# High and low weight matmuls taken in turn, block by block, in the up products of two feed-forward layers

## The chip, the cores and the metric

The kernel runs on one core of a Trainium2 chip. Its time is the device time of one execution in microseconds (us). Before the change it took 2998.19 us, the median of three executions (2997.39 to 3000.05). Every time below is of that kernel.

The matmuls go through TensorE (PE in the rows; PEld is its weight load). VectorE is DVE, ScalarE is ACT, GpSimd is POOL and SyncE, which issues the loads, is SP.

## The reference, cut to what matters

A stack of four layers runs over 256 tokens of 2048 features in float32: two of a first kind, then two of a second. Only the layers of the first kind have a feed-forward part:

```
def squared_relu_mlp(h, w_up, w_down):
    return jnp.square(jax.nn.relu(h @ w_up)) @ w_down

for layer in range(2):
    ...
    h = h + rmsnorm(mix, norm_mix_post[layer])
    f = squared_relu_mlp(rmsnorm(h, norm_mlp_pre[layer]), w_up[layer], w_down[layer])
    h = h + rmsnorm(f, norm_mlp_post[layer])
```

`w_up` is 2048 x 8192 and `w_down` 8192 x 2048. The rest (a gated mixer, a dilated attention, two layers with three kinds of attention) uses the same kind of product, and the change leaves it alone.

## The kernel before, in words

**Two halves of every number.** A float32 weight chunk is split into a rounded high part and a low part, the difference. The input is split in the same way. A product is high weight times high input, plus high weight times low input, plus low weight times high input. For each block of 128 input features (`kt`, 16 of them) that takes two matmuls:

- `high_unit` (line 306): weights `w_high`, and both halves of the input as 512 columns, into a whole bank of PSUM (`acc`).
- `low_unit` (line 313): weights `w_low`, and the high half of the input as 256 columns, added to the second half of the same bank.

VectorE then adds the two halves of the bank (`sum_halves`, line 1290), which gives the 128 output features of the chunk for 256 tokens.

**Chunks and slots.** The weights come as a stream of 512 chunks of 1 MB. Chunk c goes through slot c % 4 of `raw`, `w_high` and `w_low`. SyncE loads chunk c once product c - 4 is done. ScalarE rounds it (`high`, line 855) and VectorE subtracts (`low`, line 1281); both work three chunks ahead of the product that uses the chunk (`ahead`). TensorE waits by counters: `summed` (the bank has been read), `high_ready` and `low_ready` (the weights are split).

**The order inside a product.** `product` runs a pass over the 16 blocks with `w_high` and a pass over them with `w_low`. Without `flip` the high pass is first; with `flip` the low pass is first. In the up products of the feed-forward layers the odd slots are flipped, from the ninth product of the first quarter on, so that two low passes stand back to back and then two high passes.

**The feed-forward section.** `mlp_section` works in four quarters of the 8192 inner features. A quarter is 16 up products, one for each 128 inner features (in the first quarter four of the 16 come from an input group with wide tiles, and the next four are plain, unflipped products), and then an `out_section` of 16 wide chunks through `both_halves` (line 377), all of whose matmuls have 512 columns. After each up product VectorE adds the halves, scales, applies the squared relu and splits the result; then it does its `low` for the chunk three ahead.

The names that matter below: `product`, `high_unit`, `low_unit`, `high_ready`, `low_ready`, `summed`, `product_done`, and the call of `product` in `mlp_section`. All this order is written out by hand; no planner decides it.

Of the kernel before, what the change touches and what calls it, by code (L numbers as in the profile page):

```python
# [41 lines left out]
UNITS = 16  # L42
# [66 lines left out]
def build(nc, stream, x_t, x_rows, columns, gains_post, lambdas, w_spatial, b_spatial, positions, tables, out):  # L109
    ctx = ExitStack()  # L110
    with ctx:
# [5 lines left out]
        def sem(name):  # L117
            if name not in sems:
                sems[name] = ctx.enter_context(nc.semaphore(name))
            return sems[name]  # L120
# [115 lines left out]
        high_ready, low_ready = sem("high_ready"), sem("low_ready")  # L236
# [8 lines left out]
        def at(value):  # L245

            return max(value, 0)
# [55 lines left out]
        def _(pe):  # L303
            def high_unit(s, kt, x, bank=None, stop=False):

                return nc.tensor.matmul(acc[s if bank is None else bank][:, :], w_high[:, s, kt * P:(kt + 1) * P],  # L306
                                        x[:, kt, :, :], start=(kt == first_of[0]), stop=stop, skip_group_check=True)
# [3 lines left out]
            def low_unit(s, kt, x, stop, start=False, bank=None):  # L311

                return nc.tensor.matmul(acc[s if bank is None else bank][:, TOKENS:], w_low[:, s, kt * P:(kt + 1) * P], x[:, kt, 0, :],  # L313
                                        start=start, stop=stop, skip_group_check=True)

            def product(c, s, x, units=UNITS, hooks=None, bank=None, freed=None, order=None, flip=False):


                order = order or list(range(units))
                first_of[0] = None if flip else order[0]  # L320

                def high_pass():
                    pe.wait_ge(high_ready, c + 1)
                    for kt in order:
                        if hooks and kt in hooks:
                            hooks[kt]()
                        mm = high_unit(s, kt, x, bank, flip and kt == order[-1])
                    return mm

                def low_pass():  # L330
                    pe.wait_ge(low_ready, c + 1)
                    for kt in order:
                        mm = low_unit(s, kt, x, not flip and kt == order[-1], flip and kt == order[0], bank)
                    return mm
                pe.wait_ge(summed, at(c - 3) if freed is None else freed)
                if flip:
                    low_pass()
                    mm = high_pass()
                else:
                    high_pass()  # L340
                    mm = low_pass()
                mm.then_inc(product_done, 1)
# [126 lines left out]
            def input_group(c, n, banks, out0):  # L469


                m = n - 1
                at_turn = 4 if m % 2 and m < 4 else 1

                def first(half):
                    def ready(kt, part):
                        k = turned_at(half, kt // KT_WIDE)
                        pe.wait_ge(sem("xs_ready" if part else "xs_high"), inputs_at(n, k) - KT_WIDE + kt % KT_WIDE + 1)
                    return ready

                def second(kt, part):
                    k = turned_at(1, kt // KT_WIDE)
                    pe.wait_ge(sem("xs_ready" if part else "xs_high"), inputs_at(n, k) - KT_WIDE + kt % KT_WIDE + 1)
                pe.wait_ge(sem("rows_out"), out0 + TB * (GROUPS - 1))
                one_half(c, 0, 0, xs, banks, ready=first(0))
                one_half(c + 1, 1, 0, xs, banks, ready=first(0), hooks={at_turn: lambda: turn_rows(m, 2)})
                one_half(c, 0, 1, xs, banks, ready=first(1), hooks={at_turn: lambda: turn_rows(m, 3)}, low_last=False)\
                    .then_inc(product_done, 1)
                one_half(c + 1, 1, 1, xs, banks, ready=first(1), low_last=False,
                         hooks={4: lambda: turn_rows(m, 4), 8: lambda: turn_rows(m, 5)}).then_inc(product_done, 1)  # L490
                parts_apart(c + 2, 2, xs, banks, second,
                            hooks={8: lambda: (turn_rows(m, 6), turn_rows(m, 7))})
                parts_apart(c + 3, 3, xs, banks, second)
# [10 lines left out]
            def spread(r):  # L504

                pe.wait_ge(sem("root_ready"), r + 1)
                for n in range(TB):
                    mm = nc.tensor.matmul(extra[:, n * P:(n + 1) * P], root_of[:, n:n + 1].to_broadcast([P, P]), ident,  # L508
                                          start=True, stop=True, skip_group_check=True)
                mm.then_inc(sem("spread_done"), 1)  # L510
# [42 lines left out]
            def mlp_section(c0, split0, n, r, m, off, out0):  # L553
                def turn_up():
                    for half in range(TB):
                        pe.wait_ge(sem("up_squared"), TB * (m // 2) + half + 1)
                        for b in range(KT_WIDE):
                            mm = nc.tensor.transpose(score[half][:, b * P:(b + 1) * P],
                                                     v_four[:, half, b * P:(b + 1) * P], ident)
                        mm.then_inc(sem("up_turned"), 1)  # L560

                for q in range(FFN_QUARTERS):
                    c, before = c0 + 2 * KB * q, out0 + FINAL_GROUPS * (q - 1)
                    if q == 0:
                        input_group(c, n, (2 - off, 3 - off) if off == 0 else (0, 1), before)
                    for j in range(KT_WIDE if q == 0 else 0, KB):
                        s, hooks = j % 4, None
                        if q == 0 and j == KT_WIDE:
                            hooks = {4: lambda: spread(r)}
                        if q == 0 and j == KT_WIDE + 1:  # L570
                            hooks = {2: turn_up}
                        freed = None
                        if q == 0 and j < KT_WIDE + 2:
                            pe.wait_ge(sem("rows_out"), before + FINAL_GROUPS)
                            freed = c
                        if q and j < 4:
                            pe.wait_ge(sem("rows_out"), before + TB * (GROUPS - 1) + (TB if s > 1 else 0))
                            freed = c - KB
                        product(c + j, s, xs, bank=(s + off) % 4, freed=freed, hooks=hooks,
                                flip=s % 2 == 1 and (q > 0 or j > 7))  # L580
                    c = c + KB
                    out_section(c, m, split0 + KB * q, ((off, off + 1), (2 - off, 3 - off)), c - 2,
                                out0 + FINAL_GROUPS * q, last=q == FFN_QUARTERS - 1)

            for i, (a, b) in enumerate(FIRST_PIECES):
                last = b == KT_WIDE
                wide_high(0, 0, 0, xs, 0, units=range(a, b), high=None if last else (sem("first_high"), i + 1), xs_base=0)
                mm = wide_low(0, 0, 0, xs, 0, units=range(a, b), low=None if last else (sem("first_low"), i + 1))
# [39 lines left out]

            out_section(C_OUT0, 0, 0, ((0, 1), (2, 3)), C_OUT0 - 2, 0, MIX0_ORDER)
            mlp_section(C_MLP0, 16, 1, 1, 1, 2, FINAL_GROUPS)  # L630


# [8 lines left out]
            for i in range(HEADS // 4):  # L641
                c, off = C_QKV + 12 * i, 2 * (i % 2)
# [15 lines left out]
                for g in range(4):  # L658
                    hd, cq, s = 4 * i + g, c + 4 + 2 * g, 2 * g % 4
# [18 lines left out]
            for l in range(LAYERS):  # L678
# [25 lines left out]
                for hd in range(DA_HEADS):  # L704
                    for j in range(3):
                        p = 3 * hd + j
                        c = c0 + 4 + p
                        if p == 4:
                            pe.wait_ge(sem("v_four_ready"), TB * (HEADS // 4 + l + 1))
                        freed = c - 1 if p in (2, 3) else c - 2 if p == 5 else None  # L710
                        product(c, p % 4, xs, bank=query_banks.get(p, p % 4), freed=freed,
                                hooks={0: lambda: spread(r0)} if p == 1 else None)
# [11 lines left out]
                c, hd = c0 + N_DA, DA_HEADS - 1  # L724
# [14 lines left out]
                def window_turns(b):  # L739
                    for j in range(2):  # L740
                        turn_prob(u0 + 8 + 2 * b + j, j)
# [36 lines left out]
                c = c0 + N_DA + N_KV + N_SW  # L778
                for i in range(N_LATENT):
                    hooks = {1: {14: lambda: window_turns(SW_BLOCKS - 1)}, LATENT + 2: {4: lambda: spread(r0 + 5)}}  # L780
# [48 lines left out]
                c = c + N_LATENT  # L829
                for hd in range(MLA_HEADS):  # L830
                    hooks = {15: lambda: mla_scores(hd - 1)} if hd > 1 else {} if hd else {
                        4: lambda: latent_stat(N_LATENT - 2), 12: lambda: latent_stat(N_LATENT - 1)}
# [1332 lines left out]
```

## Time and profile before

| | |
|---|---|
| median of three executions | 2998.19 us |
| the profiled execution | 2997.29 us |
| its span on the core | 2995.3 us |
| TensorE matmul busy | 2975.1 us, 15768 matmuls |
| TensorE weight load busy | 2544.7 us |
| VectorE, ScalarE, GpSimd busy | 2033.6, 1412.1, 33.5 us |
| DMA | 554.42 MB, mean 185 GB/s |
| granted TensorE clock, whole span | 0.999 |

The busy time of TensorE is not the same as working at its peak: matmuls are pipelined, and the end of each is modelled, so that records of neighbours overlap. The distance between the starts of two matmuls is what counts. In a row of the timeline that merges n matmuls, it is the row's length less the length of one matmul, divided by n - 1; or, from one row to the next, the difference of the starts divided by the count. Weight loads overlap matmuls in the same way.

The chain of waits gives the share of each line of the work that ended last. The timeline shows the instructions in order of time. The groups by line give busy time, mean duration and the idle time ahead.

### The profile page before, as it was taken

The page shows a single profiled execution, that of the slowest core. Times are in us where ns is not written, and L with a number is a line of the kernel's source. Part 1 is how long each engine was busy: PE and PEld are TensorE (multiplying, and loading weights), DVE is VectorE, ACT ScalarE, POOL GpSimd, SP SyncE. Part 2 cuts the span into 40 slices and gives each one's busy share as a digit, 9 for nine tenths or more (in the row PEclk, how much of TensorE's full clock was granted, in tenths as well). Part 3 has the DMA queues.
Part 4 walks back from the last instruction along what each step waited for, and adds up shares of the span by engine and source line. Part 5 has one row for each costly group of instructions (what it writes and reads, how often), then busy time and mean ns, then how long its engine had stood idle before and what let it go on. Part 6 is the DMA issues. An engine that isn't in the chain of part 4 may idle for free.

```text
span 2995.3 us, 38044 instructions
## 1 busy us (share of the span) xinstructions
PE 2975.1 (99%) x15768; PEld 2544.7 (85%) x15768; DVE 2033.6 (68%) x2720; ACT 1412.1 (47%) x1798; POOL 33.5 (1%) x38
## 2 busy tenths in 40 slices
PE   9999999999999999999999999999999999999999
PEld 7888888888888788888888888888888888888887
DVE  7776765746566587775756657465689865789764
ACT  5334543434333465554533334343666644666543
POOL 0000000000000000000000000000000000000000
PEclk9999999999999999999999999999999999999999
DMA  7555455555555444445555555555444445444444
GB/s 267 215 184 204 175 189 191 194 189 192 195 186 210 171 181 170 177 180 192 182 188 191 194 188 195 193 187 211 170 168 169 156 159 193 182 172 152 169 157 166
DMA packets 81658, 554.42 MB, mean 185 GB/s; under 512 B 9040, under 2 KB 9552, under 8 KB 16080
## 3 DMA queue, kind: packets, MB, share of 16 engines
q1 hardware_dynamic: 81488, 552.00, 50.9%
q8 instruction: 125, 2.05, 0.3%
q14 instruction: 45, 0.37, 0.0%
HBM read 549.87 MB, written 2.10 MB: 184 GB/s over the span
## 4 chain that ended last, share of the span: by engine, by line
PE 97%; issue 1%; ACT 1%; DVE 1%; POOL 0%; DMA 0%; SPq 0%; DVEq 0%; POOLq 0%; ACTq 0%
PE acc L377 37%; PE acc L306 33%; PE acc L313 17%; PE acc L356 2%; PE score L518 2%; PE acc L366 1%; PE acc L802 1%; PE head_out L547 1%; PE score L526 1%; PE acc L809 1%; PE head_out L549 0%; PE score L436 0%; DMA raw<-stream 0%; PE extra L508 0%; DVE w_low L1281 0%
## 5 line engine op out<-in xcount | busy, mean ns | idle before, releaser
L1281 DVE TENSOR_TENSOR w_low<-raw,w_high 128x2048 fp32r<-128x2048 f32 x511 | 1163.9, 2280 | 537.2 <-ACT w_high L855 536.3
L855 ACT ACTIVATE w_high<-raw 128x2048 fp32r<-128x2048 f32 x511 | 974.7, 1909 | 1158.3 <-DMA raw<-stream 1158.0
L306 PE MATMUL acc<-xs,w_high 128*128 128x512 f32 x4322 | 1039.4, 393 | 0.0
L306 PEld LDWEIGHTS acc<-xs,w_high 128*128 128x128 f32 x4322 | 795.6, 188 | 163.5 <-issue 6.0
L377 PE MATMUL acc<-w_high,inner 128*128 128x512 f32 x3072 | 733.6, 390 | 0.0
L377 PEld LDWEIGHTS acc<-w_high,inner 128*128 128x128 f32 x3072 | 575.4, 188 | 118.6
L313 PEld LDWEIGHTS acc<-xs,w_low 128*128 128x128 f32 x4322 | 544.7, 191 | 15.5
L313 PE MATMUL acc<-xs,w_low 128*128 128x256 f32 x4322 | 549.5, 283 | 0.0
L377 PE MATMUL acc<-w_low,inner 128*128 128x512 f32 x1536 | 382.5, 390 | 0.0
L1290 DVE TENSOR_REDUCE y<-acc 128x256 f32<-128x512 f32 x272 | 187.5, 689 | 254.6 <-PE acc L313 148.9
L377 PEld LDWEIGHTS acc<-w_low,inner 128*128 128x128 f32 x1536 | 287.8, 188 | 60.2 <-issue 0.7
L935 ACT ACTIVATE inner<-source 128x256 fp32r<-128x256 f32 x168 | 69.8, 415 | 93.4 <-DVE source L1456 57.8
L987 ACT ACTIVATE swapped<-y 32x256 f32<-32x256 f32 (+1 forms) x208 | 86.5, 416 | 39.2 <-DVE y L1290 36.6
L994 ACT ACTIVATE prob<-prob,small 128x128 f32<-128x128 f32 (+1 forms) x144 | 64.5, 449 | 69.0 <-DVE small L1533 37.7
L1298 DVE TENSOR_TENSOR scaled<-y,scale_pre 128x256 f32<-128x256 f32 x192 | 81.6, 425 | 9.8
L356 PE MATMUL acc<-w_high,xs 128*128 128x512 f32 x320 | 80.4, 402 | 6.9 <-ACT w_high L1021 6.5
L377 PE MATMUL acc<-w_high,xs 128*128 128x512 f32 x320 | 82.9, 397 | 0.0
L356 PEld LDWEIGHTS acc<-w_high,xs 128*128 128x128 f32 x320 | 60.2, 192 | 19.6 <-ACT w_high L1021 6.5
L1420 DVE TENSOR_TENSOR inner<-source,inner 128x256 fp32r<-128x256 f32 x168 | 70.2, 418 | 1.0 <-ACT inner L935 1.0
L377 PEld LDWEIGHTS acc<-w_high,xs 128*128 128x128 f32 x320 | 58.3, 188 | 13.3 <-issue 1.9
L1456 DVE SCALAR_TENSOR_TENSOR source<-scaled 128x256 f32<-128x256 f32 x120 | 51.0, 425 | 4.1
L1361 DVE SCALAR_TENSOR_TENSOR xs<-score,col,xs 128x128 fp32r<-128x128 f32 x120 | 33.7, 343 | 18.5 <-ACT xs L877 18.5
(177 smaller groups left out, 1401.9 us busy)
## 6 DMA issues: line engine op xcount, KB each, us to landing
raw<-stream SPq DMA_DIRECT2D x511, 1024.0 KB, 4.8
gain<-gains_post SPq DMA_DIRECT2D x24, 256.0 KB, 5.0
h<-x_rows SPq DMA_DIRECT2D x8, 256.0 KB, 5.1
out<-h SPq DMA_DIRECT2D x8, 256.0 KB, 2.1
x_in<-x_t SPq DMA_DIRECT2D x3, 512.0 KB, 9.8
consts<-tables SPq DMA_DIRECT2D x1, 960.0 KB, 15.7
x_in<-x_t SPq DMA_DIRECT2D x2, 256.0 KB, 4.3
raw<-stream SPq DMA_DIRECT2D x2, 256.0 KB, 4.4
```

The costliest lines, as they stand in the source:

```text
L306: return nc.tensor.matmul(acc[s if bank is None else bank][:, :], w_high[:, s, kt * P:(kt + 1) * P], x[:, kt, :, :], start=(kt == first_of ...
L313: return nc.tensor.matmul(acc[s if bank is None else bank][:, TOKENS:], w_low[:, s, kt * P:(kt + 1) * P], x[:, kt, 0, :], start=start, sto ...
L356: mm = nc.tensor.matmul(acc[bank + n][:, :], x[:, kt, part, n * P:(n + 1) * P], w_high[:, s, a * WIDE:(a + 1) * WIDE], start=(kt == 0 and ...
L377: return nc.tensor.matmul(acc[bank][:, :], x[:, kt, part, rows(n)], w[:, s, a * WIDE:(a + 1) * WIDE], start=start, stop=stop, skip_group_c ...
L855: nc.scalar.activation(w_high[:, s, 0:units * P], raw[:, s, 0:units * P], ACT.Copy)\
L935: nc.scalar.activation(inner[:, b, 0], source[:, s, :], ACT.Copy).then_inc(sem("inner_high"), 1)
L987: cp = nc.scalar.activation(to[a:a + half, :], src[b:b + half, :], ACT.Copy)
L994: nc.scalar.activation(prob[:, bank, lo:hi], prob[:, bank, lo:hi], ACT.Exp, bias=neg_max(bank, t), accum_out=denom(bank, t)).then_inc(sem( ...
L1281: V.tensor_tensor(w_low[:, s, 0:units * P], raw[:, s, 0:units * P], w_high[:, s, 0:units * P], ALU.subtract).then_inc(low_ready, 1)
L1290: V.tensor_reduce(y[:, s % 2, :], acc[s if bank is None else bank][:, :].rearrange("p (a t) -> p t a", a=2), AXIS_X, ALU.add)\
L1298: V.tensor_tensor(to, y[:, s % 2, :], scale, ALU.mult).then_inc(sem(done), 1)
L1420: V.tensor_tensor(inner[:, b, 1], source[:, s, :], inner[:, b, 0], ALU.subtract)\
```

## The change

`product` gets a new argument, `mixed`. With it, the product waits for the bank and for both parts of the weights at its start, and then issues the high matmul and the low matmul of each input block in turn, 16 times. The call in `mlp_section` passes `mixed` where it could pass `flip` before, and for the even slots of the same stretch too: from the ninth product of the first quarter on, and in all of the three quarters behind. That is 8 + 3 x 16 = 56 products in each of the two layers, 112 in all, with 1792 high and 1792 low matmuls. No product of a feed-forward layer is flipped any more. The number of matmuls, their shapes and operands stay the same.

```diff
-            def product(c, s, x, units=UNITS, hooks=None, bank=None, freed=None, order=None, flip=False):
+            def product(c, s, x, units=UNITS, hooks=None, bank=None, freed=None, order=None, flip=False, mixed=False):
...
                 pe.wait_ge(summed, at(c - 3) if freed is None else freed)
-                if flip:
+                if mixed:
+                    pe.wait_ge(high_ready, c + 1)
+                    pe.wait_ge(low_ready, c + 1)
+                    for kt in order:
+                        high_unit(s, kt, x, bank)
+                        mm = low_unit(s, kt, x, kt == order[-1], bank=bank)
+                elif flip:
                     low_pass()
                     mm = high_pass()
...
                         product(c + j, s, xs, bank=(s + off) % 4, freed=freed, hooks=hooks,
-                                flip=s % 2 == 1 and (q > 0 or j > 7))
+                                mixed=q > 0 or j > 7)
```

TensorE before, in the first feed-forward layer: the end of the last plain product of the first quarter, the ninth product, and the tenth, which is flipped (`acc` is the bank, `xs` the input).

```order
L313 MATMUL acc<-xs,w_low 128x256 x15
L306 MATMUL acc<-xs,w_high 128x512 [waits high_ready,summed]
L306 MATMUL acc<-xs,w_high 128x512 x15
L313 MATMUL acc<-xs,w_low 128x256 [waits low_ready]
L313 MATMUL acc<-xs,w_low 128x256 x15
L313 MATMUL acc<-xs,w_low 128x256 [waits low_ready,summed]
L313 MATMUL acc<-xs,w_low 128x256 x15
L306 MATMUL acc<-xs,w_high 128x512 [waits high_ready]
L306 MATMUL acc<-xs,w_high 128x512 x15
```

TensorE now, from the same place.

```order
L313 MATMUL acc<-xs,w_low 128x256 x15
L306 MATMUL acc<-xs,w_high 128x512 [waits low_ready,high_ready,summed]
L313 MATMUL acc<-xs,w_low 128x256
L306 MATMUL acc<-xs,w_high 128x512
L313 MATMUL acc<-xs,w_low 128x256
```

What stood in runs of 16 or 32 of one width now changes width at every matmul, and the wait for `low_ready` has moved from the product's middle to its start.

TensorE before, where the last up product of a quarter (flipped) meets the first wide product of the down part (`inner` is the squared relu's result).

```order
L313 MATMUL acc<-xs,w_low 128x256 [waits low_ready,summed]
L313 MATMUL acc<-xs,w_low 128x256 x15
L306 MATMUL acc<-xs,w_high 128x512 [waits high_ready]
L306 MATMUL acc<-xs,w_high 128x512 x15
L377 MATMUL acc<-w_high,inner 128x512 [waits inner_ready,high_ready,summed]
```

TensorE now, at the same place.

```order
L306 MATMUL acc<-xs,w_high 128x512
L313 MATMUL acc<-xs,w_low 128x256
L306 MATMUL acc<-xs,w_high 128x512
L313 MATMUL acc<-xs,w_low 128x256
L383 MATMUL acc<-w_high,inner 128x512 [waits inner_ready,high_ready,summed]
```

The up part now ends with a low matmul, where it ended with 16 high ones; line 377 is now line 383. The instructions of the other engines and of SyncE keep their order.

## Rows read from the trace of the kernel before

**Rows 1.** The page: busy time, and the chain of waits by engine and line.

```profile
PE 2975.1 (99%) x15768; PEld 2544.7 (85%) x15768; DVE 2033.6 (68%) x2720; ACT 1412.1 (47%) x1798; POOL 33.5 (1%) x38
...
PE 97%; issue 1%; ACT 1%; DVE 1%; POOL 0%; DMA 0%; SPq 0%; DVEq 0%; POOLq 0%; ACTq 0%
PE acc L377 37%; PE acc L306 33%; PE acc L313 17%; PE acc L356 2%; PE score L518 2%; PE acc L366 1%; PE acc L802 1%; PE head_out L547 1%; PE score L526 1%; PE acc L809 1%; PE head_out L549 0%; PE score L436 0%; DMA raw<-stream 0%; PE extra L508 0%; DVE w_low L1281 0%
```

**Rows 2.** Chain of waits, in order of time: start us, us, what.

```profile
506.24 3.63 PE acc L306 x16
509.87 3.83 PE acc L313 x32
513.70 7.28 PE acc L306 x32
520.98 3.83 PE acc L313 x32
524.81 7.28 PE acc L306 x32
...
595.14 87.04 PE acc L377 x384
```

**Rows 3.** Stretches: two up products; TensorE's clock is PEclk, (x) counts instructions.

```profile
core 0: us, PE busy (x) PEld busy (x) DVE busy (x) ACT busy (x) POOL busy (x), PEclk, DMA share, GB/s
382.04:393.15 11.11, 11.11 (x66) 9.84 (x65) 8.16 (x11) 4.67 (x5) 0.00 (x0) 1.00 0.54 194
```

**Rows 4.** Timeline of PE: start us, us, engine line, tiles, shape, count.

```profile
378.21 4.00 PE L313 MATMUL acc<-xs,w_low 128*128 128x256 f32 x32
382.04 7.44 PE L306 MATMUL acc<-xs,w_high 128*128 128x512 f32 x32
389.32 4.00 PE L313 MATMUL acc<-xs,w_low 128*128 128x256 f32 x32
```

**Rows 5.** Timeline of PE: single high matmuls behind the low ones that end at 382.04.

```profile
382.04 0.40 PE L306 MATMUL acc<-xs,w_high 128*128 128x512 f32 x1
382.27 0.40 PE L306 MATMUL acc<-xs,w_high 128*128 128x512 f32 x1
382.51 0.39 PE L306 MATMUL acc<-xs,w_high 128*128 128x512 f32 x1
...
383.20 0.39 PE L306 MATMUL acc<-xs,w_high 128*128 128x512 f32 x1
```

**Rows 6.** Timeline of PE: one low matmul between high ones, in a layer behind.

```profile
2253.66 0.28 PE L313 MATMUL acc<-xs,w_low 128*128 128x256 f32 x1
2253.78 2.46 PE L306 MATMUL acc<-xs,w_high 128*128 128x512 f32 x10
```

**Rows 7.** Timeline of PE: low matmuls behind one, two and four high ones.

```profile
2445.95 0.50 PE L306 MATMUL acc<-xs,w_high 128*128 128x512 f32 x1
2446.29 2.08 PE L313 MATMUL acc<-xs,w_low 128*128 128x256 f32 x16
...
2276.74 0.71 PE L306 MATMUL acc<-xs,w_high 128*128 128x512 f32 x2
2277.28 2.06 PE L313 MATMUL acc<-xs,w_low 128*128 128x256 f32 x16
...
2416.72 1.18 PE L306 MATMUL acc<-xs,w_high 128*128 128x512 f32 x4
2417.74 1.47 PE L313 MATMUL acc<-xs,w_low 128*128 128x256 f32 x11
```

**Rows 8.** Timeline of PE: eight transposes of 128 columns, each with its weight load.

```profile
357.44 1.03 PE L558 MATMUL score<-consts,v_four 128*128 128x128 f32 x8
```

**Rows 9.** Timeline of DVE: the split of weights beside the up products.

```profile
381.85 2.28 DVE L1281 TENSOR_TENSOR w_low<-raw,w_high 128x2048 fp32r<-128x2048 f32 x1
...
496.69 2.29 DVE L1281 TENSOR_TENSOR w_low<-raw,w_high 128x2048 fp32r<-128x2048 f32 x1 [1.31 <-ACT w_high L855]
```

**Rows 10.** Groups by line, 506.1 to 595.1 us: busy us, mean ns, idle before.

```profile
L306 PE MATMUL acc<-xs,w_high 128*128 128x512 f32 x256 | 59.7, 390 | 0.0
L313 PE MATMUL acc<-xs,w_low 128*128 128x256 f32 x256 | 32.0, 283 | 0.0
```

## The prediction

> **What bounds the kernel now.** I read the page first. Matmuls are busy for 99% of the span, and the chain of work that ended last is TensorE for 97%; lines 306 and 313, the two that the change reorders, are 33% and 17% of it [rows 1]. VectorE and ScalarE have room (68% and 47%). So only TensorE's own pace, or a wait that newly stops it, can move the time.
>
> The groups by line of one quarter's up part, 506.1 to 595.1 us, come next. Lines 306 and 313 have 256 matmuls each there and no idle time ahead of them [rows 10]. The up part never waits. What is to be predicted is the distance from one matmul's start to the next.
>
> The chain in order of time gives these distances: 384 matmuls of 512 columns in 87.04 us, 0.2267 us each; 32 high ones in 7.28 us, 0.2275 each; 32 low ones in 3.83 us, 0.1197 each [rows 2]. A pair of products, 32 of each, takes 11.11 us at granted clock 1.00, the 2.4 GHz level [rows 3]. So one high and one low matmul together now cost 11.11 / 32 = 0.3473 us. The change has 1792 such pairs (112 products of 16), 622 us of the span. One nanosecond per pair is 1.8 us of the whole.
>
> **What a change of width costs now.** From the settled runs, 512 columns take 0.2267 and 256 columns 0.1200 ((4.00 - 0.28) / 31 in the low rows [rows 4]). The difference, 0.1067 for 256 columns, is 0.417 ns a column, so both widths carry the same 13 ns on top of their columns. That speaks for a cost per matmul that does not care what stands next to it: in turn, a pair would then be 0.2267 + 0.1200 = 0.3467.
>
> But the settled pace is not kept at a change of width. A run of 32 high matmuls behind low ones starts at 382.04 and the low ones at 389.32: 7.28 us, where 32 x 0.2267 is 7.25. The missing 0.03 us is at the front of the run: the first starts are 382.04, 382.27, 382.51, and the sixth is 383.20 [rows 5]. The first two distances are about 0.235, and the five together 1.16, 0.232 each. Five high matmuls pass before the pace is settled. In the new order no high matmul ever has five high ones ahead of it; all 1792 stand where the first of such a run stands.
>
> The low matmul has a small gain at the same place. 32 of them behind high ones take 3.83 where 32 x 0.1200 is 3.84 [rows 4]. Behind short runs of high ones I read (2.08 - 0.28) / 15 = 0.120 (one high), (2.06 - 0.28) / 15 = 0.1187 (two), (1.47 - 0.28) / 10 = 0.119 (four) [rows 7]. One low matmul alone between high ones exists: it starts at 2253.66, the next high one at 2253.78, 0.12 later to the rounding of the row, and the ten high ones behind go at (2.46 - 0.39) / 9 = 0.230 [rows 6].
>
> **The change part by part.**
>
> 1. The pairs in turn. The high one costs between 0.2267 (settled) and 0.2355 (the first two of [rows 5]). I take 0.231, between the 0.232 of the first five there and the 0.230 behind the lone low one. The low one costs between 0.109 and 0.120. The lower end is from the transposes, the shortest matmuls that carry a weight load of this size: eight in 1.03 us, (1.03 - 0.27) / 7 = 0.109, so a load can repeat that fast [rows 8]. I take 0.1185, by the short runs. The sum is 0.3495 against 0.3473: +2.2 ns, x 1792 = +4.0 us. The ends are 0.2267 + 0.109 = 0.3357, or -20.8 us, and 0.2355 + 0.120 = 0.3555, or +14.7 us. Both parts of this step are from rows of changes that come once, not at every matmul, and that is the main doubt.
>
> 2. The changes between passes that go. Each pair of products loses one low-to-high and one high-to-low change, but they are inside the 0.3473 already: nothing more to count.
>
> 3. The ends of the quarters. The up part ended with high matmuls and ran into the 384 wide ones without a change of width; now it ends with a low one. Eight such places at the 0.03 us of a run's front: +0.2 us.
>
> 4. The wait for both parts of the weights at a product's start. Before, the even products needed `w_low` only after their high pass, 16 x 0.227 = 3.6 us in. VectorE splits three chunks ahead. The product that ends in the middle of the low run, at 378.21 + 3.83 / 2 = 380.13, is followed by the split that starts at 381.85 and ends at 384.13 [rows 4, 9]; that one is for the third product behind, which starts two products of 5.56 later, at 391.24: 7.1 us of lead. The first product of a quarter starts at 506.1 and its low part is done at 496.69 + 2.29 = 498.98 [rows 9]: 7.1 us again. The new wait comes where this lead is counted from, so it costs nothing. Each product that found the cover gone would stop for up to 3.6 us. The flipped products needed `w_low` at the start already and show no idle time [rows 10].
>
> 5. Nothing moves on the other engines. Products end when they did, so SyncE's loads, which wait for `product_done`, and VectorE's sums keep their places.
>
> The sum is +4.2 us on the profiled execution: 2997.3 becomes 3001.5. The median of the runs lies 0.9 us above the profiled one, so I forecast 3002 us.
>
> The weight load is where a rule speaks for the change. Two low matmuls that follow each other leave 0.120 for a load, and the rows show loads repeating in 0.109 at best [rows 8]; settled high matmuls take 0.2267 though they leave twice the room. So in these rows the surplus of 13 ns does not come from a lack of room for the load. The Trainium skill (TensorE: Matmul & The Clock Gate, "Back-to-back issue gap") gives the distance of bare matmuls at the full clock as N / 2.4 + 2.5 ns, and says that with weight loads the spacing is set by both operations, pipelined through a queue that pulls loads ahead. By that page alone, an estimate: a pair of 215.8 + 109.2 = 325 ns if the loads, spread over long and short matmuls, vanish behind them. The trace does not agree for the settled runs: 226.7 ns stands where the page has 216, with a load as well hidden as it can be.
>
> **The rivals.**
>
> - The slower side, "every high matmul is a first one": an unsettled start costs 0.2355 each time, as twice in [rows 5], and the low ones gain nothing. A pair is 0.3555, +14.7 us, 3013 us. For it: the new order is the unsettled place without end. Against it: the third of that run is already at about 0.23, and behind the lone low one the mean is 0.230. It decides from 0.3507 a pair on (+6 us).
> - The faster side, "the load hides in the long matmul": each low one follows a high one in whose time its weights came in, and leaves after about 0.114 (half way from 0.109 to 0.1185), and the high one keeps 0.2267. A pair is 0.3407, -11.8 us, 2986 us. For it: the 0.01 us that a low run gains at its front. Against it: the low ones in [rows 7] keep 0.119 to 0.120 behind high ones.
> - The loads vanish behind both widths. From rows: columns alone for the high one, 512 x 0.417 ns = 0.2133, and 0.1115 for the low one give 0.3248, -40 us, 2958 us. The page's rule above ends at the same place. Against it: 384 wide matmuls in a row keep 0.2267 [rows 2]. (The page's rule above would bring the time to the same place.)
> - Nothing but the lengths: 0.3467 a pair, -1 us, 2997 us.
>
> **How the numbers follow.** A difference under 0.2%, 6 us, can't be told from no change here. The forecast (a pair of 0.348 to 0.352) has 0.42, of which 0.05 lies over 6 us; nothing but the lengths has 0.07; the slower rival 0.30; the faster one 0.18; both widths 0.03. That gives faster 0.21, same 0.44, slower 0.35. The range of 8 in 10 is 2984 to 3015: it takes in the middle of the faster rival and the whole price of the slower one, and leaves out the 3% at 2958, the far end of the low matmul's gain, and anything dearer than all the rows. The forecast's own range is 2998 to 3008.
>
> **What would show it.** In the new profile the up part should still show no idle time ahead of lines 306 and 313. The 16 products of a quarter, 506 to 595 us, took 16 x 5.556 = 88.9 us; at 0.3495 a pair they take 89.5, at 0.3555 they take 91.0, at 0.3407 they take 87.2. High matmuls whose mean duration rises from 390 ns towards 396 to 398 would say that they are all unsettled, and low ones that fall under 283 ns that the load hides. The forecast is wrong in its mechanism if a wait on `low_ready` shows up in front of a product, and wrong in size if the pair lies outside 0.348 to 0.352. Stretches without up products should keep their lengths.

## The result, and the profile after

The changed kernel takes 3009.56 us (median of 6 executions, 3008.25 to 3011.07), against 2998.06 us for the kernel before in the same comparison (6 executions, 2997.02 to 3000.05). The ratio is 1.0039, with a 95% interval of 1.0028 to 1.0051: slower by 0.4%, 11.5 us. The forecast was 3002 us, with 2998 to 3008 as its own range and 2984 to 3015 as the range of 8 in 10; the slower rival had been put at 3013 us.

The page after, its busy times, the share of the chain and two groups by line, to be held against [rows 1]:

```profile
PE 2986.1 (99%) x15768; PEld 2542.4 (85%) x15768; DVE 2034.6 (68%) x2720; ACT 1412.1 (47%) x1798; POOL 33.5 (1%) x38
...
PE 97%; issue 1%; ACT 1%; DMA 1%; DVE 0%; POOL 0%; SPq 0%; DVEq 0%; POOLq 0%; ACTq 0%
...
L306 PE MATMUL acc<-xs,w_high 128*128 128x512 f32 x4322 | 1254.8, 397 | 0.0
...
L313 PE MATMUL acc<-xs,w_low 128*128 128x256 f32 x4322 | 829.0, 282 | 0.0
```

TensorE is still the chain, with the same number of matmuls and no idle time ahead of the two lines. VectorE's and ScalarE's work is the same within a microsecond or so. The busy times of lines 306 and 313 have risen from 1589 to 2084 us together, but that is how overlapping records add up when the two lines alternate; the page's PE total rose only by 11.0 us.

Where the time went can be read from the chain in order of time. These are the runs of 384 wide matmuls, one behind each of three quarters; the columns are start us, us, what, as in [rows 2]:

```profile
421.58 87.05 PE acc L383 x384
...
599.07 87.06 PE acc L383 x384
776.58 87.06 PE acc L383 x384
```

From one such run to the next the kernel takes 776.58 - 599.07 = 177.51 us. Take off the run's 87.06 and divide by the 256 pairs of the quarter: **0.3533 us a pair**, against 0.3473 before. 1792 pairs at 6.0 ns make 10.8 us. (Unless it is said otherwise, this division gives the pair in the experiments below.)

The groups by line of one up part, 508.7 to 599.0 us, are the counterpart of [rows 10]:

```profile
L306 PE MATMUL acc<-xs,w_high 128*128 128x512 f32 x256 | 90.5, 399 | 0.0
L313 PE MATMUL acc<-xs,w_low 128*128 128x256 f32 x256 | 71.9, 281 | 0.0
```

The mean high matmul went from 390 to 399 ns, more than the 396 to 398 that the prediction gave for "all unsettled"; the mean low one from 283 to 281. The chain inside the up part shows the pattern that the pair has found:

```profile
509.32 0.24 PE acc L306
509.56 0.12 PE acc L313
509.68 0.23 PE acc L306
509.92 0.12 PE acc L313
510.03 0.23 PE acc L306
510.26 0.12 PE acc L313
510.38 0.24 PE acc L306
```

Look at the starts of the high matmuls: 509.32, 509.68, 510.03, 510.38. They make a round of three pairs, 1.06 us, and the quarter as a whole keeps its pace, 0.3533 us a pair. It does not settle to 0.3467.

The trace's difference is larger (3008.1 - 2995.3 = 12.8 us of span), and most of the rest is not the change's. The first load of weights landed later; before and after:

```profile
4.08 9.18 DMA raw<-stream
```

```profile
4.08 10.84 DMA raw<-stream
```

That is 1.7 us. This load differs from run to run: it took 8.86 to 10.19 us in the kernels of the experiments, which all begin in the same way. The ends of the quarters take the 0.02 us that 87.06 stands over 87.04 in [rows 2].

### The profile page after: what moved, and what is told of

Read it like the earlier page. It is cut to its first block, busy times and chain, and to the rows that moved or that the text cites. A ratio compares the mean times of both kernels' runs of the same rounds, so it can differ in the third digit from the quotient of the medians.

```text
span 3008.1 us, 38068 instructions
## 1 busy us (share of the span) xinstructions
PE 2986.1 (99%) x15768; PEld 2542.4 (85%) x15768; DVE 2034.6 (68%) x2720; ACT 1412.1 (47%) x1798; POOL 33.5 (1%) x38
## 4 chain that ended last, share of the span: by engine, by line
PE 97%; issue 1%; ACT 1%; DMA 1%; DVE 0%; POOL 0%; SPq 0%; DVEq 0%; POOLq 0%; ACTq 0%
PE acc L383 37%; PE acc L306 33%; PE acc L313 17%; PE acc L362 2%; PE score L524 2%; PE acc L372 1%; PE acc L808 1%; PE head_out L553 1%; PE score L532 1%; DMA raw<-stream 1%; PE acc L815 1%; PE head_out L555 0%; PE score L442 0%; PE extra L514 0%; ACT w_high L861 0%
## 5 line engine op out<-in xcount | busy, mean ns | idle before, releaser
L306 PE MATMUL acc<-xs,w_high 128*128 128x512 f32 x4322 | 1254.8, 397 | 0.0
L313 PE MATMUL acc<-xs,w_low 128*128 128x256 f32 x4322 | 829.0, 282 | 0.0
L313 PEld LDWEIGHTS acc<-xs,w_low 128*128 128x128 f32 x4322 | 660.8, 190 | 11.4
## 6 DMA issues: line engine op xcount, KB each, us to landing
x_in<-x_t SPq DMA_DIRECT2D x3, 512.0 KB, 11.5
```

## The experiments

The question after the result was what makes a pair dearer by 6.7 ns than its two settled lengths (0.3467). I held three theories against each other.

- **Short slot**: the weight load that falls under the 256-column matmul is late for the long matmul behind it.
- **Width change**: any change of width between neighbours unsettles the pace.
- **Operands**: the bank's half that has just been written, or the two weight tiles in turn.

All but the runs of two were executed once. Several of the kernels add or leave out products, so their whole time says nothing of the order, and the pair is what is compared. The times were 3105.77 us (low matmuls of 384 columns), 3056.22 (320), 3188.76 (512), 2814.31 (both 256) and 3095.87 (384 in passes).

**Low matmuls into the other half of the bank.**

```diff
+            def low_wide(s, kt, x, stop, bank, n=256):
+                x_flat = x[:, kt, :, :].rearrange("p a t -> p (a t)")
+                return nc.tensor.matmul(acc[s if bank is None else bank][:, 0:n], w_low[:, s, kt * P:(kt + 1) * P],
+                                        x_flat[:, 0:n], start=False, stop=stop, skip_group_check=True)
...
-                        mm = low_unit(s, kt, x, kt == order[-1], bank=bank)
+                        mm = low_wide(s, kt, x, kt == order[-1], bank)
```

> The changed kernel, with the low matmul's 256 columns added into the first half of the bank where they went into the second (the two halves are summed afterwards, so the result is the same number). A settled high and low matmul make 0.3467 us a pair; in the changed kernel the pair takes 0.3533. Theory 'short slot' (the weight load that falls under the 256-column matmul is late for the long matmul behind it) and theory 'width change' (any change of width costs) expect 0.3533 again. Theory 'bank' (the low matmul adds to columns that the high one has only just written) expects the pair to move: towards 0.3467, since the columns 0 to 255 were written 0.11 us earlier.

Measured: the wide runs start at 597.77 and 775.27, so a quarter takes 177.50 us and a pair 0.3533. The one execution beside the kernel before took 3008.62 against 2997.71 us. The half of the bank plays no part.

**Low matmuls of 384 columns**: the same edit with `n=384`.

> High and low in turn, the low matmul 384 columns wide (it adds low weight times low input for half of the tokens). A settled matmul costs 13.3 ns over its columns, so a pair without surplus is 0.2267 + 0.1733 = 0.4000 us. 'Short slot' expects 0.4000, since 0.17 us hold a weight load with room to spare. 'Width change' expects the surplus of 6.7 ns to stay: 0.4067. 'Two weight tiles' (w_high and w_low, or their operands, taken in turn) expects 0.4067 too.

Measured, the chain's wide runs of three quarters:

```profile
427.73 87.09 PE acc L389 x384
618.92 87.05 PE acc L389 x384
810.06 87.05 PE acc L389 x384
```

(810.06 - 618.92 - 87.05) / 256 = 0.4066 us a pair: the surplus is 6.6 ns. In the first quarter, whose in-turn part follows low matmuls, it is larger (in both layers), by the chain there:

```profile
419.88 0.24 PE acc L306
420.11 0.18 PE acc L319
420.29 0.24 PE acc L306
...
423.60 0.24 PE acc L306
```

Nine pairs in 3.72 us are 0.4133 each, a surplus of 13.3 ns. So "short slot" falls: with 0.17 us of room for the load, the surplus is as large or twice as large. The same code keeps one of two paces as long as the stretch lasts. The slower one stands behind low matmuls and the faster one behind settled 512-column matmuls; that this is the cause is the likeliest reading, but no run changed it alone.

**Both 512 columns wide**: the same edit with `n=512`.

> High and low in turn, both 512 columns wide (the low one adds low weight times low input for all tokens). Without surplus a pair is 0.4533 us. 'Short slot' and 'width change' both expect 0.4533. 'Two weight tiles' expects 0.46.

```profile
636.85 87.04 PE acc L389 x384
839.94 87.04 PE acc L389 x384
```

(839.94 - 636.85 - 87.04) / 256 = 0.4533: no surplus at all, with `w_high` and `w_low` in turn. With the first run, in which the bank's other half changed nothing, "operands" falls.

**Both 256 columns wide.**

```diff
-                        high_unit(s, kt, x, bank)
+                        nc.tensor.matmul(acc[s if bank is None else bank][:, 0:TOKENS], w_high[:, s, kt * P:(kt + 1) * P],
+                                         x[:, kt, 0, :], start=kt == order[0], stop=False, skip_group_check=True)
```

> High and low in turn, both 256 columns wide: the products that are taken in turn leave out high weight times low input. Without surplus a pair is 0.2400 us. 'Width change' expects 0.2400. 'Short slot' expects 0.2400 as well, since low matmuls in a row keep 0.1200 and there is no long one to disturb. 'Two weight tiles' expects 0.2467.

```profile
499.89 0.12 PE acc L340
500.01 0.12 PE acc L313
...
501.09 0.12 PE acc L340
```

Five pairs in 1.20 us, 0.2400 each: no surplus. The quarter as a whole comes to (705.48 - 555.23 - 87.07) / 256 = 0.2468, which happens to be what "two weight tiles" expected, but its surplus is not spread over the pairs. In the trace, 482 of the 502 distances between starts from 494 to 555 us are 0.120, and six are 0.19 to 0.27. They stand at the starts of products, where the waits are; what these stops wait for, the trace doesn't name. Together with the run before: equal widths, none; unequal widths, always some. "Width change" is what is left.

**Passes of 16 with low matmuls of 384 columns**, in the order of the kernel before.

```diff
-                        mm = low_unit(s, kt, x, not flip and kt == order[-1], flip and kt == order[0], bank)
+                        if wide:
+                            mm = low_wide(s, kt, x, not flip and kt == order[-1], flip and kt == order[0], bank)
+                        else:
+                            ...
...
-                                flip=s % 2 == 1 and (q > 0 or j > 7))
+                                flip=s % 2 == 1 and (q > 0 or j > 7), wide=q > 0 or j > 7)
```

> The order of the kernel before (passes of 16, every second product flipped), with low matmuls of 384 columns in the 112 products: the comparison for the run with 384 columns in turn, which took 0.4066 us a pair in three quarters of the up part and 0.4133 in the first. If a settled matmul costs 13.3 ns over its columns at this width too, the pair is 0.4000, and with the fronts of the runs (20 ns in 32 pairs) 0.4006; then the surplus of the order in turn is that of its changes alone. If low matmuls of 384 columns are themselves slower than 0.1733, the surplus belongs to the width.

The timeline of a settled stretch, and two neighbours of its chain:

```profile
519.31 2.41 PE L319 MATMUL acc<-xs,w_low 128*128 128x384 f32 x13
```

```profile
516.50 5.57 PE acc L319 x32
522.07 7.29 PE acc L306 x32
```

(2.41 - 0.334) / 12 = 0.173: the settled matmul carries 13 ns over its columns at this width as well, so the surplus of the order in turn was not the width's own. But 32 of them take 5.57 where 32 x 0.1733 is 5.55, and the pair over a quarter is (805.78 - 615.81 - 87.04) / 256 = 0.4021, not 0.4006. Between 512 and 384 columns the low run pays at its front too, where a 256-column run gains. Held against these passes, the order in turn costs 4.5 ns a pair at this width (0.4066).

**Low matmuls of 320 columns in turn**: `n=320`.

> High and low in turn, the low matmul 320 columns wide. Settled lengths make 0.2267 + 0.1467 = 0.3733 us a pair. 'Short slot' has fallen at 384 columns already (it left a surplus of 6.6 to 13.3 ns there). 'Width change' expects 0.3800 or 0.3867, by the state in which a stretch starts: behind a run of 512 columns the lower one, behind low matmuls the higher one. A surplus that shrinks in proportion to the difference of widths would give 0.3783.

The wide runs start at 607.71 and 792.04 and take 87.07: (184.33 - 87.07) / 256 = 0.3799, a surplus of 6.6 ns. The first quarters keep the same pace here, though they too follow low matmuls, so the second state of the 384-column run did not come back. The price is not in proportion to the difference of widths, which would give 0.3783.

**Runs of two.**

```diff
-                    for kt in order:
-                        high_unit(s, kt, x, bank)
-                        mm = low_unit(s, kt, x, kt == order[-1], bank=bank)
+                    for k in range(0, units, 2):
+                        for kt in order[k:k + 2]:
+                            high_unit(s, kt, x, bank)
+                        for kt in order[k:k + 2]:
+                            mm = low_unit(s, kt, x, kt == order[-1], bank=bank)
```

> Two high matmuls, then two low ones, in the 112 products (shapes as in the changed kernel). Settled lengths make 0.3467 us a pair, one and one in turn 0.3533. Theory 'each round' (a round high to low to high costs 6.7 ns, however long its runs are) expects 0.3500 a pair, so +4.8 us on the kernel before. Theory 'front of five' (each high run pays what the kernel before pays at the front of its runs, 6.6, 9.1, 1.7, 5.8 and 4.1 ns, and each low run gains 7.5 ns at its front) expects (6.6 + 9.1 - 7.5) / 2 = +4.1 ns, 0.3508, so +6 us.

Measured, with wide runs that start at 595.99 and 772.20: (772.20 - 595.99 - 87.05) / 256 = 0.3483 us a pair, under both theories (0.3500 and 0.3508). In time it can't be told from the kernel before: 2999.77 us (10 executions, 2999.26 to 3002.28) against 2998.52 us (13 executions), ratio 1.0005 (0.9996 to 1.0015). The chain shows why it is cheap:

```profile
520.05 0.47 PE acc L306 x2
520.52 0.23 PE acc L313 x2
520.75 0.46 PE acc L306 x2
521.22 0.23 PE acc L313 x2
```

Two high ones cost 0.46 to 0.47 where settled ones take 0.453, but two low ones take only 0.23 where settled ones take 0.24.

**Runs of four.** The same edit with 4.

> Runs of four high and four low matmuls. 'Each round' expects 0.3483 us a pair (+1.9 us on the kernel before). 'Front of five' expects (6.6 + 9.1 + 1.7 + 5.8 - 7.5) / 4 = +3.9 ns, 0.3506 (+6 us).

```profile
520.08 0.93 PE acc L306 x4
521.00 0.48 PE acc L313 x4
521.48 0.93 PE acc L306 x4
522.41 0.47 PE acc L313 x4
```

(775.53 - 598.66 - 87.09) / 256 = 0.3507, as "front of five" had it, and dearer than runs of two. One execution took 3006.16 us.

**Runs of eight.** The same edit with 8.

> Runs of eight high and eight low matmuls. Measured so far: 0.3533 us a pair in turn, 0.3483 in runs of two, 0.3507 in runs of four, 0.3473 in the passes of before. 'Front of five' expects (27.3 - 7.5) / 8 = +2.5 ns over 0.3467, 0.3492. 'Each round' in its fallen form (a price that the length of the runs does not set) has no number left; under 0.3480 would fit it better.

(772.16 - 595.73 - 87.07) / 256 = 0.3491: "front of five" again (0.3492). One execution took 3000.56 us. So the surplus over 0.3467 by the length of a run is 6.6 ns (one), 1.6 (two), 4.0 (four), 2.4 (eight) and 0.6 (the runs of 32 of before). From four on it is what the front of a long run costs, shared out; at one and two that sum does not give the price. No order tried is faster than the kernel before.

**Half a weight load for the low matmuls.** The last question was where the 13 ns come from that every settled matmul carries. Two kernels load only 64 of 128 weight columns for the low matmuls. First in passes:

```diff
+            def low_half(s, kt, x, stop, start=False, bank=None, m=P // 2):
+                return nc.tensor.matmul(acc[s if bank is None else bank][0:m, TOKENS:], w_low[:, s, kt * P:kt * P + m],
+                                        x[:, kt, 0, :], start=start, stop=stop, skip_group_check=True)
...
-                        mm = low_unit(s, kt, x, not flip and kt == order[-1], flip and kt == order[0], bank)
+                        unit = low_half if half and not (flip and kt == order[0]) else low_unit
+                        mm = unit(s, kt, x, not flip and kt == order[-1], flip and kt == order[0], bank)
```

> The order of the kernel before, with low matmuls that load 64 weight columns where they loaded 128 (in the 112 products, all but the first low matmul of a flipped one): they leave out the low weights of the upper 64 features of each chunk. It asks where the 13.3 ns come from that each settled matmul costs over its columns. If they come with the weight load that runs under it, a settled low matmul with half the load beside it takes less than 0.1200, about 0.1133. If they are a fixed price of a matmul, it stays 0.1200.

The timeline of the settled part of a low pass (a merged row; one matmul is 0.276 us by the groups of the same stretch):

```profile
531.74 1.41 PE L318 MATMUL acc<-xs,w_low 128*64 128x256 f32 x11
```

(1.41 - 0.276) / 10 = 0.113 us against 0.120 with the full load: with half the load the surplus over the columns falls from 13 to about 6.7 ns. A quarter's pair is (767.73 - 593.33 - 87.04) / 256 = 0.3413; the kernel took 2986.95 us against 2998.67 for the kernel before (one execution of each). These low matmuls also fill only half of the output rows, so this run alone can't tell the load's price from the matmul's own. Then in turn (the same `low_half`, called in the `mixed` branch):

> High and low in turn with the same half weight loads for the low matmuls (the low weights of the upper 64 features of each chunk are left out). The half load is the one that runs under the high matmul. If the load takes its time from the matmul beside it, the pair falls from 0.3533 to about 0.3467, and the high matmul's own distance falls. If the surplus of the changed order is a matter of widths alone, the pair stays 0.3533.

```profile
595.15 87.07 PE acc L388 x384
770.96 87.07 PE acc L388 x384
```

(770.96 - 595.15 - 87.07) / 256 = 0.3466 us a pair against 0.3533: 6.7 ns less again (one execution: 2996.48 against 2998.67 us). What decides is which of the two matmuls got faster, and the chain shows it:

```profile
507.10 0.23 PE acc L306
507.33 0.12 PE acc L318
507.44 0.23 PE acc L306
507.67 0.12 PE acc L318
...
509.87 0.23 PE acc L306
```

Over the eight pairs from 507.10 to 509.87 the high distances average 0.229 and the low ones 0.117. In the changed kernel they were 0.237 and 0.117. So the gain is all in the high matmul, which is itself unchanged but has the half load beside it; the low matmul, which is the narrower one, gained nothing. (The mean duration of the high one says the same: 392 ns, where the changed kernel has 399.) That is the price of the load, paid in the settled stretches by the matmul that streams beside it: 13 ns for 128 columns, 6.7 for 64. That all of the 13 ns would go without a load is that proportion carried on; no kernel without loads was run. Nor does the saving show at once at a change of width: in the kernel with passes, where a half load runs under the last high matmul of a pass, that one still takes 0.226 (531.05 to 531.27 in the trace), and the low ones behind it 0.118, 0.116 and 0.114. The surplus of the order in turn seems to be there still: half the 13 ns off the settled 0.3467 would be 0.3400, an estimate, and 0.3466 was measured.

## Why the prediction was right or wrong

**What bounds the kernel**: right. No wait appeared, and the change's time is in the distance between starts on lines 306 and 313, but for the quarters' ends.

**The numbers against the prediction's own signs.** The measured 3009.6 us lies inside the range of 8 in 10. It lies outside the forecast's own range (2998 to 3008), and the pair, 0.3533, lies outside 0.348 to 0.352, which the prediction had named as the sign that its size is wrong. The range held because it had been drawn wide enough for the slower rival, which the pair bears out (it decides from 0.3507 on).

**Step 1, the pairs in turn**: the kind of cost was right, its size was not. I had +2.2 ns a pair; it is +6.0, and that term alone is 10.8 of the 11.5 us. In the round of the chain above, from 509.32 to 510.38, the three high distances are 0.24 + 0.24 + 0.23 = 0.71, the three low ones 0.12 + 0.11 + 0.12 = 0.35. So the low matmul was near (0.1185 taken, 0.117 measured) and the high one failed (0.231 taken, 0.237 measured): I took 0.231, as the mean of a run's first five, and wrote myself that all 1792 stand where the first of such a run stands. The first two of [rows 5] cost 0.235; two of three in the new order cost 0.24 to the rounding of the row. The later ones of the front, which brought my mean down, are matmuls that have had high ones ahead of them, which the new order never gives. The row behind the lone low matmul (0.230) had the same flaw: nine distances between ten high ones in a row.

Taking only the first matmul of each run would have missed too. The first high one of [rows 5] goes in 0.23. The first low one of a run has its own price, by the chain of the kernel before, read in windows that keep single matmuls apart:

```profile
520.98 0.12 PE acc L313
...
521.09 0.12 PE acc L313
...
521.21 0.12 PE acc L313
```

From the starts, the first low one takes 0.11 and the second 0.12; over all the runs of 32 in the trace the firsts average 0.2333 (high) and 0.1133 (low). Together that is 0.3467, no surplus at all, where 0.3533 was measured. What failed is the step itself: a price read at a change that comes once in a run was taken as the price of a change that comes at every matmul. The prediction had called this its main doubt.

**Step 2 and step 3**: the quarters' ends cost 0.01 to 0.02 us each where I had 0.03. Step 2 is only bookkeeping, and nothing speaks against it.

**Step 4, the wait for both parts**: right. Lines 306 and 313 have no idle time ahead of them in the up part.

**Step 5**: right as far as it was looked at. The distances outside the up parts stayed: the wide runs take 87.05 or 87.06 where they took 87.04.

**The surplus of 13 ns**: I argued that it does not come from a lack of room for the load, and that was right, but I left open what it is. The half loads show it: it comes with the load all the same, as time that the load takes from the matmul beside it. Settled matmuls of 256, 384 and 512 columns with a load of 128 columns beside them took 13 ns over their columns alike, and no order tried lowered that. That also answers the faster rivals. By the Trainium skill (TensorE: Matmul & The Clock Gate, "Back-to-back issue gap") a bare matmul of N columns takes N / 2.4 + 2.5 ns at the full clock. No run here reached that, since each matmul had a load beside it, and none tests it, since no kernel without loads was run.

**The rivals**: "every high matmul is a first one" was the nearest, with 0.3555 a pair and 3013 us; measured were 0.3533 and 3009.6. It had 0.30, the forecast 0.42. Its price for the high one (0.2355) was near the mean of 0.237, though its name doesn't fit: it is above what a first one costs (0.233). It gave the low one no gain, and it has 3 ns. In the rival in which the loads vanish behind both widths, no row gives the 0.1115 of the low matmul; its columns alone are 0.1067, which would make 0.3200 a pair and about -49 us. Measured at 0.3533, it is out with either.

**What stays open**: what the state is that a change of width disturbs. The runs show that equal widths don't disturb it, that it takes about five 512-column matmuls to settle, that 384 columns can hold either of two paces, and that the price by length of run is 6.6, 1.6, 4.0, 2.4, 0.6 ns. Whether the surplus of the order in turn would go if there were no weight loads was not tried.

## What to carry to other kernels

Where TensorE runs without a gap, count starts per pair, not busy time, and prefer long runs of one width: here passes of 16 gave 0.3473 us a pair, one and one in turn 0.3533. The price does not fall evenly with the length of the run (two cost less than four), so a short run has to be measured.

A distance read at a place that comes once in a run is a price for that place only. Neither the mean of a run's front nor its first matmul gave the price of an order that repeats the change at every step: the one would have 0.3495, the other 0.3467. Keep the range open there, since the repeated order may find a round of its own.

A weight load that is "hidden" still costs its neighbour time. Halving the load of the low matmuls (with a part of the product left out) took about 6 ns off a pair in passes, where no order of the whole loads took anything off.

## What the runs showed of the hardware that I had not expected

- With a weight load of 128 columns beside it, a settled matmul takes 13 ns over its columns at each of three widths (0.120, 0.173 and 0.2267 us for 256, 384 and 512 columns at 0.417 ns a column); with one of 64 columns, 6.7 ns (0.113 for 256 columns). In turn, the half load made the high matmul beside it faster (0.237 to 0.229) and left the low one that it belongs to at 0.117.
- Matmuls of 512 and 256 columns in turn did not settle within a quarter: three pairs repeat as a round of 1.06 us, 20 ns over the settled lengths. At equal widths (512 and 512, 256 and 256) there was no surplus.
- The same pattern can keep one of two paces for as long as it lasts: 512 and 384 columns in turn kept 0.4066 us a pair behind wide matmuls and 0.4133 behind low ones. 512 and 320 columns had one pace, 0.3799, in both places.
